# First four FFN units on x times scale, shift and root at their eviction, and two units' split weights in other buffers

## The reference

```
h = rms_norm(x) * (1 + scale) + shift        # scale, shift: per feature, from mod = silu(c) @ mod_w + mod_b
x = x + 0.5 * gate * ((silu(h @ w_g) * (h @ w_u)) @ w_down)      # D_FF = 2816
```

## Time and profile before

| | us |
|---|---|
| median of 3 runs | 1985.31 (1983.57 to 1985.61) |
| the profiled execution's own time | 1985.01 |
| span in the profile | 1983.2 |
| TensorE busy | 1952.4 |
| VectorE busy | 1138.5 |
| ScalarE busy | 716.8 |
| POOL busy | 214.1 |
| start of the first four units / of units 8 and 9 | 20.15 / 72.85 |

### The profile page before, as it was taken

The page is one execution under the profiler, slowest core; times in us unless marked ns, Lnnn a source line. Parts: engine busy times, 40 slices in busy tenths (PEclk is TensorE's granted clock), DMA queues, the critical chain, the costliest instruction groups (busy, mean ns, idle before and its releaser), DMA issues.

```text
span 1983.2 us, 23246 instructions
## 1 busy us (share of the span) xinstructions
PE 1952.4 (98%) x8990; PEld 1619.5 (82%) x8990; DVE 1138.5 (57%) x1692; ACT 716.8 (36%) x1056; POOL 214.1 (11%) x246
## 2 busy tenths in 40 slices
PE   7999999999999999999999999999999999999998
PEld 5888888888888888888888888878888888888886
DVE  7665564799857655645864453586554572433334
ACT  5322222464743213224422221356465442222123
POOL 4110100017701100100110000001111000000000
PEclk9999999999999999999999999999999999999999
DMA  8665552322016655622554543223322233323221
GB/s 318 236 219 170 202 191 96 103 90 88 33 64 223 203 183 187 232 83 87 175 200 136 166 159 108 93 98 112 97 85 86 70 104 97 106 85 106 85 90 59
DMA packets 75197, 263.94 MB, mean 133 GB/s; under 512 B 8770, under 2 KB 8898, under 8 KB 75123
## 3 DMA queue, kind: packets, MB, share of 16 engines
q1 hardware_dynamic: 54720, 190.87, 28.7%
q0 software_dynamic: 20256, 72.02, 11.0%
q10 hardware_dynamic: 146, 0.09, 0.0%
HBM read 260.66 MB, written 2.13 MB: 133 GB/s over the span
## 4 chain that ended last, share of the span: by engine, by line
PE 94%; DVE 3%; POOL 1%; issue 1%; ACT 1%; DMA 0%; SPq 0%; DVEq 0%; ACTq 0%; POOLq 0%
PE bank L1392 29%; PE bank L1397 29%; PE bank L1393 29%; PE bank L1800 1%; DVE dve_tmp L953 1%; PE bank L1817 1%; PE bank L1732 1%; PE bank L1576 1%; DVE h_lo L944 1%; PE bank L1578 1%; PE bank L1577 1%; PE bank L1789 0%; PE bank L1707 0%; PE bank L1456 0%; DVE wlo L816 0%
## 5 line engine op out<-in xcount | busy, mean ns | idle before, releaser
L1392 PE MATMUL bank<-h_hi,whi 128*128 128x512 f32 x1808 | 711.5, 394 | 7.5 <-DVE wlo L816 4.5
L1393 PE MATMUL bank<-h_hi,wlo 128*128 128x512 f32 x1808 | 705.5, 390 | 0.0
L1397 PE MATMUL bank<-h_lo,whi 128*128 128x512 f32 x1808 | 593.9, 390 | 0.5 <-POOL h_lo L378 0.5
L481 ACT ACTIVATE whi<-wraw 128x1024 fp32r<-128x1024 f32 x338 | 347.0, 1053 | 267.0 <-PE bank L1397 263.9
L816 DVE TENSOR_TENSOR wlo<-wraw,whi 128x1024 fp32r<-128x1024 f32 x324 | 389.0, 1224 | 59.9 <-ACT whi L481 59.6
L1392 PEld LDWEIGHTS bank<-h_hi,whi 128*128 128x128 f32 x1808 | 340.7, 188 | 81.0 <-issue 6.1
L1397 PEld LDWEIGHTS bank<-h_lo,whi 128*128 128x128 f32 x1808 | 340.1, 188 | 73.1 <-POOL h_lo L378 1.2
L1393 PEld LDWEIGHTS bank<-h_hi,wlo 128*128 128x128 f32 x1808 | 340.8, 189 | 68.9
L1392 PE MATMUL bank<-hid_hi,whi 128*128 128x512 f32 x832 | 324.3, 390 | 0.0
L1397 PE MATMUL bank<-hid_lo,whi 128*128 128x512 f32 x832 | 323.7, 389 | 0.0
L1393 PE MATMUL bank<-hid_hi,wlo 128*128 128x512 f32 x832 | 323.7, 389 | 0.0
(11 more groups left out here) (237 smaller groups left out, 1351.3 us busy)
## 6 DMA issues: line engine op xcount, KB each, us to landing
wraw<-in_w_units_dram SPq DMA_DIRECT2D x306, 512.0 KB, 3.5
arena<-in_mod_t_dram POOLq DMA_DIRECT2D x96, 512.0 KB, 5.0
mod_tile<-in_mod_t_dram POOLq DMA_DIRECT2D x32, 512.0 KB, 4.8
wraw<-in_w_units_dram SPq DMA_DIRECT2D x32, 384.0 KB, 3.6
arena<-in_mod_t_dram SPq DMA_DIRECT2D x12, 512.0 KB, 8.1
arena<-in_w_units_dram SPq DMA_DIRECT2D x10, 512.0 KB, 4.5
xT<-in_xt_dram SPq DMA_DIRECT2D x8, 256.0 KB, 4.5
sq<-k_roots POOLq DMA_DIRECT2D x8, 256.0 KB, 3.5
```

The lines of the kernel that those rows point to most:

```text
L481: act.activation(whi[:, s % RING, :, :], wraw[:, s % RING, :, :], ACT.Copy).then_inc(hi_ready, 1)
L1392: pe.matmul(dst, whi[:, w, k, :], hi_, start=first, stop=False)
L1393: pe.matmul(dst, wlo[:, w, k, :], hi_, start=False, stop=False)
L1397: return pe.matmul(dst, whi[:, s % RING, k, :], lo_, start=False, stop=last)
```

## The change

1. `first_tile`: all 8 scale columns come first, then the 8 shift columns.
2. Units 0 to 3 run on x * scale without root and shift: ScalarE makes the rounded product (`first_scaled`, L535 of the new file), VectorE its lower part (`first_lower`, L1186). The root is spread by TensorE between the matmuls of these units, behind the part of units 0 and 1 for k = 2, and ScalarE copies it to `ssum` after its fourth scaled column.
3. The shift goes through the weights of units 0 to 3 by 16 matmuls with a 2-row output (L1714), turned into columns by four small ones (L1733). At eviction VectorE multiplies the bank by the root (`first_evict`, L1198); the shift column is the bias of the gate function (L568) and is added in the product (L1080).
4. Units 4 and 5 keep their split weights in the upper halves of `hid_hi` and `hid_lo` (L554 on ScalarE, L388 on POOL, L1227 on VectorE) and have matmuls of their own (`first_pair`), step by step with the pieces of h.
5. h itself is made after that, from `ssum` in place of the bank, with a new buffer in the arena. Units 6 and 7 are raised after it (ScalarE) and split within the gating of hidden tile 1 (VectorE).
6. On TensorE the second pair of pairs in each FFN's first third is written out, and the loop starts one later.

```diff
@@
-    return KT * (1 - t % 2) + t // 2
+    return KT + t if t < KT else t - KT
@@ POOL
+            first_lo(2)
+            first_lo(3)
+            pool.wait_ge(hi_ready, 5)
+            pool.wait_ge(lo_ready, 4)
+            pool.tensor_tensor(first_lo_[0], wraw[:, 0, :, :], first_hi[0].bitcast(F32), ALU.subtract).then_inc(lo_ready, 1)
             for k in range(KT):
-                if k == 1:
-                    first_lo(2)
-                    first_lo(3)
                 pool.wait_ge(h_rounded, k + 1)
-                pool.tensor_tensor(h_lo[:, k, :], sq[:, k % 2, :], h_hi[:, k, :].bitcast(F32), ALU.subtract)\
+                pool.tensor_tensor(h_lo[:, k, :], first_full[k % 2], h_hi[:, k, :].bitcast(F32), ALU.subtract)\
                     .then_inc(h_ready, 1)
@@ ScalarE
             hi(0)
+            first_scaled(0)
             hi(1)
-            first_h(0)
+            first_scaled(1)
             hi(2)
             hi(3)
-            for k in range(1, KT):
+            for k in range(2, KT):
+                first_scaled(k)
+                if k == 3:
+                    act.wait_ge(rb_ready, 1)
+                    act.activation(ssum[:, :], bank[RB], ACT.Copy).then_inc(rb_kept, 1)
+            first_raised(0)
+            first_raised(1)
+            for k in range(KT):
                 first_h(k)
+            act.wait_ge(rows_done, 1)
+            hi(6)
+            hi(7)
             act.wait_ge(mod_done, MOD_FIRST)
             act.activation(cond[:, :], cond_wide, ACT.Copy).then_inc(cond_kept, 1)
             ffn(0, 1)
@@ VectorE, gating of the first FFN
+                        elif f == t == 0 and n < 2:
+                            dve.wait_ge(evicted, s + 2)
+                            dve.wait_ge(shift_kept, 1)
+                            dve.scalar_tensor_tensor(out=dve_tmp[:, n, :], in0=first_out[2 * n + 1],
+                                                     scalar=shift_out[:, 2 * n + 1:2 * n + 2], in1=act_tmp[:, n, :],
+                                                     op0=ALU.add, op1=ALU.mult).then_inc(early_gated, 1)
+                            if n:
+                                lo(6)
+                                lo(7)
@@ VectorE, the start
+            for k in range(2, KT):
+                mod_column(k)
+                dve.wait_ge(mod_done, k + 1)
+                first_lower(k)
+            for t in range(KT, MOD_FIRST):
+                mod_column(t)
+            dve.wait_ge(mod_done, MOD_FIRST)
+            link(dve.tensor_copy(shift_split[:, :, 0], modc[:, 0:KT]))
+            dve.tensor_tensor(shift_split[:, :, 1], modc[:, 0:KT], shift_split[:, :, 0].bitcast(F32), ALU.subtract)\
+                .then_inc(first_shift, 1)
+            dve.wait_ge(rb_kept, 1)
+            first_evict(0)
+            first_evict(1)
             first_norm(0)
-            lo(0)
-            lo(1)
+            dve.wait_ge(hi_ready, 6)
+            dve.wait_ge(lo_ready, 5)
+            dve.tensor_tensor(first_lo_[1], wraw[:, 1, :, :], first_hi[1].bitcast(F32), ALU.subtract).then_inc(lo_ready, 1)
             for k in range(1, KT):
-                mod_column(2 * k)
-                mod_column(2 * k + 1)
                 first_norm(k)
...
+            first_evict(2)
+            first_evict(3)
+            dve.wait_ge(columns_done, 1)
+            dve.tensor_copy(shift_out[:, :], bank[OB][:, 0:4]).then_inc(shift_kept, 1)
+            dve.wait_ge(h_ready, KT)
             dve.wait_ge(cond_kept, 1)
             ffn(0, 1)
@@ TensorE
                         if f == 0:
                             first_units()
+                            first_pair()
+                            pair(6, 0, (2, 3), 4)
                         else:
                             up_body(up, 0, True)
-                        with pe.Fori(0, k // 2 - 1) as i:
-                            up_body(up + 4, i, False)
+                            up_body(up + 4, 0, False)
+                        with pe.Fori(0, k // 2 - 2) as i:
+                            up_body(up + 8, i, False)
@@ TensorE, first_units
                 for k in range(KT):
                     last = part(0, k)
-                    if k:
-                        part(2, k - 1)
                     if k == KT - 1:
                         last.then_inc(unit_done, 2)
+                    if k == 2:
+                        pe.wait_ge(root_ready, 1)
+                        spread(bank[RB], 0, 0).then_inc(rb_ready, 1)
+                    if k:
+                        part(2, k - 1).then_inc(early_used, 1)
                 part(2, KT - 1).then_inc(unit_done, 2)
+                pe.wait_ge(first_shift, 1)
...
```

More of the change, by code:

```diff
@@ L517, in round_h, with first_scaled @@
                                    scale=1.0).then_inc(h_rounded, 1)
+            def first_scaled(k):
+                act.wait_ge(mod_done, k + 1)
+                act.activation(h_hi[:, k, :], xT[:, k, :], ACT.Copy, scale=modc[:, KT + k:KT + k + 1]).then_inc(early_rounded, 1)
             def first_h(k):
@@ L537, in up_body @@
                             s = up + 2 * q
+                            if f == 0 and s < RING and isinstance(i, int):
+                                act.wait_ge(evicted, s + 1)
+                                act.wait_ge(shift_kept, 1)
+                                act.activation(act_tmp[:, q, :], first_out[2 * q], ACT.Silu,
+                                               bias=shift_out[:, 2 * q:2 * q + 1], scale=1.0).then_inc(act_out, 1)
+                                act.wait_ge(early_gated, q + 1)
+                                act.activation(hid_hi[:, q:q + 1, :], dve_tmp[:, q:q + 1, :], ACT.Copy)\
+                                    .then_inc(hid_rounded, 1)
+                                continue
                             if early and q == 0:
@@ L1127, in _, with first_lower @@
             dve.wait_ge(cond_spread, 1)
-            mod_column(0)
-            mod_column(1)
-            spread_rstd(0)
+            def first_lower(k):
+                dve.wait_ge(early_rounded, k + 1)
+                dve.scalar_tensor_tensor(out=h_lo[:, k, :], in0=xT[:, k, :], scalar=modc[:, KT + k:KT + k + 1],
+                                         in1=h_hi[:, k, :].bitcast(F32), op0=ALU.mult, op1=ALU.subtract)\
+                    .then_inc(early_ready, 1)
             def first_norm(k):
-                dve.wait_ge(mod_done, 2 * k + 2)
                 if k >= 2:
@@ L1136, in first_norm, with first_evict @@
                 dve.scalar_tensor_tensor(out=dve_tmp[:, k % 2, :], in0=xT[:, k, :], scalar=modc[:, KT + k:KT + k + 1],
-                                         in1=bank[RB][:, :], op0=ALU.mult, op1=ALU.mult).then_inc(normed, 1)
+                                         in1=ssum[:, :], op0=ALU.mult, op1=ALU.mult).then_inc(normed, 1)
+            def first_evict(n):
+                dve.wait_ge(unit_done, n + 2 - n % 2)
+                dve.tensor_tensor(first_out[n], bank[n], ssum[:, :], ALU.mult).then_inc(evicted, 1)
+            mod_column(0)
+            dve.wait_ge(stat_done, 1)
+            dve.tensor_scalar(var[:, 0, 0:NB], bank[OB][:, 0:NB], 1.0 / D, EPS, ALU.mult, ALU.add).then_inc(var_ready, 1)
+            lo(0)
+            dve.wait_ge(mod_done, 1)
+            first_lower(0)
+            lo(1)
+            mod_column(1)
+            dve.wait_ge(mod_done, 2)
+            first_lower(1)
+            split_roots(0, NB)
+            for k in range(2, KT):
[11 more added lines that the diff above has]
+            first_evict(1)
             first_norm(0)
-            lo(0)
-            lo(1)
+            dve.wait_ge(hi_ready, 6)
+            dve.wait_ge(lo_ready, 5)
+            dve.tensor_tensor(first_lo_[1], wraw[:, 1, :, :], first_hi[1].bitcast(F32), ALU.subtract).then_inc(lo_ready, 1)
             for k in range(1, KT):
-                mod_column(2 * k)
-                mod_column(2 * k + 1)
                 first_norm(k)
+                if k == 4:
+                    dve.wait_ge(rows_done, 1)
+                    dve.tensor_copy(first_rows, bank[OB][0:2, :]).then_inc(rows_kept, 1)
+            first_evict(2)
[3 more added lines that the diff above has]
+            dve.wait_ge(h_ready, KT)
             dve.wait_ge(cond_kept, 1)
@@ L1592, in first_stat @@
                 ins.then_inc(stat_done, 1)
-                pe.wait_ge(root_ready, 1)
-                spread(bank[RB], 0, 0).then_inc(rb_ready, 1)
             def first_units():
@@ L1608, in first_units, with first_pair @@
                     last = part(0, k)
-                    if k:
-                        part(2, k - 1)
                     if k == KT - 1:
                         last.then_inc(unit_done, 2)
-                part(2, KT - 1).then_inc(unit_done, 2)
+                    if k == 2:
[3 more added lines that the diff above has]
+                        part(2, k - 1).then_inc(early_used, 1)
+                part(2, KT - 1).then_inc(unit_done, 2)
```

(25 more changed lines are left out.)

34 lines of the change are left out of this document (25 added, 9 removed).

## The result

The changed kernel takes 2003.11 us (median) where the kernel before, run beside it, takes 1984.44: a ratio of 1.0092, 95% interval 1.0081 to 1.0103, or 18.7 us more. One single run of the six took 9706.79 us and is no part of the ratio. The profiled execution took 2003.35 us, with a span of 2001.6.

What follows compares the result with a forecast made beforehand. TensorE, busy 98%, bounds the kernel through its stands and slow matmuls. Units 8 and 9 begin at 30.5 + 48.8 + 10.9 + 2.5 = 92.7 against 72.85, +19.9 us, so 2005.0 us, range 1998.5 to 2010.5.

Steps and rivals of the forecast that it cites:

- the likeliest case: The chain waits for the splits of units 6 and 7, and VectorE and POOL hold each other: 2005.0 us, chance 0.60.
- T: End of the root's spread on TensorE: 32.8 at the slow level, 29.3 at the fast, taken as 30.5 us.
- stand before the shift's matmuls: TensorE, done with units 0 to 3, stands near 4 us; this decides nothing, as the chain runs on through VectorE.
- wait for the first modulation tile: VectorE before its modulation columns: POOL fetches the tile after its last h_lo, landing 4.9 us after issue, at T + 43.3.
- What starts earlier: Kernel start: TensorE begins near 17.4 instead of 20.15, but units 2 and 3 wait for POOL's splits until 25.6.
- The new chain: From the root's spread through VectorE's columns and shift split to the last h_lo: T + 20.2, then T + 38.4.
- I therefore add VectorE's and POOL's work instead of laying it side by side: Making the eight pieces of h: both engines hold each other, 14.3 us from T + 24.0, done 3.6 us later.
- The rival without holding: VectorE and POOL do not hold each other while making h: +16.0 us, 2001.0 us; chance 0.22.
- The tail: After h: gate, two modulation columns, second product, then VectorE's splits of units 6 and 7, done at T + 48.8.
- The slow level after the long stand: TensorE on units 6 and 7 after standing over 9 us: slow matmuls cost 2.5 us, bounds 0 and 4.4.
- TensorE is the bound after all: Rival: only TensorE's own work counts up to units 8 and 9, +1.3 us, 1986.5 us; chance 0.03.

Runs made afterwards that it cites:

- experiment two: Changed kernel with ScalarE's copy of the root moved behind its last scaled column, nothing else: 1999.01 us, 4.1 us under the changed kernel.
- Experiment one: Changed kernel with VectorE's splits of units 6 and 7 moved ahead of the first gate, nothing else: 1998.36 us, 4.75 us under the changed kernel.
- five to eight: Includes one run not named singly: experiment three plus modulation columns of the first two tiles moved behind the third gate's splits: 1988.89 us, ratio 1.002.
- experiment five: Changed kernel with 30 extra matmuls, read by nothing, on TensorE right ahead of units 6 and 7: 2000.51 us, 2.6 us under the changed kernel.
- experiment seven: Experiment three plus columns of tiles 0 and 1 behind the third gate's splits, and the norm reading the root from its bank: 1987.61 us, ratio 1.0014.
- experiment eight: Changed kernel with units 4 and 5 split into the ring's own buffers, as before the change: 2012.17 us, 9.1 us over the changed kernel.
- experiment three: Changed kernel with both splits of 6 and 7 ahead of the first gate and the root's copy behind the scaled columns: 1991.82 us, ratio 1.0037.
- experiment four: Changed kernel with the norm of the first h reading the root from its bank, not SBUF: 2003.12 us, ratio 1.0093.
- kernel nine: Experiment seven with VectorE's column k+1 ahead of the lower part of k, and the root's split ahead of lower part 1: 1985.47 us, ratio 1.0006.
- ten: Kernel nine with TensorE taking the root's spread and units 0 and 1's third part before units 2 and 3's first part: 1982.71 us, ratio 0.999.

## Why the prediction was right, and where its terms were off

The forecast was 2005.0 (1998.5 to 2010.5), the result 2003.11; the likeliest case is the one that happened. Step by step, with T the end of the root's spread:

| term | predicted | measured |
|---|---|---|
| TensorE begins | 17.4 | 17.22 |
| units 2 and 3's splits | 25.6 | 25.34, after a stand of 3.76 |
| T | 30.5 | 31.5 |
| split of the shift | T + 20.2 | T + 20.6 |
| stand before the shift's matmuls | near 4 | 4.21 |
| last h_lo done | T + 38.4 | T + 37.2 |
| wait for the first modulation tile | 0.8 (T + 42.5 to 43.3) | none, column at T + 41.5 |
| splits of units 6 and 7 done | T + 48.8 | T + 46.9 |
| units 6 and 7 | 10.9 + 2.5 slow | 12.45, so 10.9 + 1.55 |
| units 8 and 9 begin | 92.7 | 90.97 |

- **What starts earlier** held to 0.3 us, with POOL's splits as the limit.
- **The new chain** held. Its hand-overs made a column 2.81 us and not 2.72, which for three columns is 0.3 of the 0.4. That the stand before the shift decides nothing was right: experiment two takes it away, and what it wins is the chain's 5.0 us, as VectorE's splits, not TensorE, are last.
- **T** was mis-sized by 1.0. I had put it nearer to the fast end; in the changed kernel TensorE was at the fast level from 19.95 to the stand of 3.76 us, and the 12 matmuls behind that stand ran at 0.43 but for the last. Part of this is the execution that was traced. In the profiles of one, two and five to eight all of the first 12 matmuls ran at 0.43, the stand was 2.63 us or so, the first 3 to 6 matmuls behind it were fast, and T came 13.6 us after the first matmul; in the changed kernel's, three's, four's and nine's the fast level came before the stand, and T 14.3 to 14.8 after the first matmul. With 13.6 T would have been 30.8. Why a start goes one way or the other stays open.
- **"I therefore add VectorE's and POOL's work instead of laying it side by side"** had the right mechanism (experiments four and eight) and the wrong size. Seven steps took 1.72 us each, not the 1.96 of adding 1.29 and 0.67. It is less than the full sum, 1.2 us in all. Two things were missing: the norm costs 0.4 to 0.55 us beside POOL and not 0.67 (experiment eight's steps, and the 0.55 by which each norm outlasts POOL's piece), and the pace is that of the ring of two pieces, in which it counts once in two steps. In the record of the changed kernel it stands as a longer VectorE instruction (1.78), hardly as a longer one of POOL. The Trainium skill, page "SBUF — State Buffer", section "SBUF: two separate sides", names this holding; by its rule alone the sum would be mine. The rows bear out that the two are coupled, that in experiment eight either can be the one that waits, and that reading the root from the bank frees them; and they show that a step is shorter than the whole sum. The rival without holding, 2001.0, would have needed steps of 1.36; with the bank they are 1.48, as the ring of ScalarE and POOL then limits, which the prediction did not have.
- **The tail** held by order: gate, two columns, gate, splits. Experiment one is worth 7.5 us at that place: 2.6 of the 3.1 us for which VectorE waited for the gate function, and the 5.1 from there to the splits at 76.11, less 0.25 by which the first split ran longer (1.47 for 1.22). The tile landed within 4.35 us of POOL's issue at 68.69, and no column waited; I had taken 4.9.
- **The slow level after the long stand**, 2.5 predicted, measured 1.55 in the trace and 1.4 by experiment five. It came back 2.8 us after the start, not 5. The page "TensorE: Matmul & The Clock Gate", section "Part 1: The HAM clock gate" of the Trainium skill gave the direction, which experiment five confirms; without it 2.5 would have been left out, and the sum would have been 1.55 us too low in place of 0.95 too high at this step.
- **"TensorE is the bound after all"** was rightly small. But its sum, +1.3, was no floor: ten reaches -2.2, since with the spread and a third part ahead of POOL's splits the 3.1 us of waiting shrink to 0.9, and only 10 matmuls run slowly (2.1 us, where I had 4).

The errors cancel in part: +1.0 at T, -1.9 in the chain (1.2 of it h, the rest the tile and hand-overs), -0.95 at the clock, together some -1.8 at units 8 and 9. The medians differ by 18.7 us where the two traces differ by 18.1 at the mark.

## What to carry to other kernels

When a product is made free of a late factor (here the root, pulled to the eviction), look where the factor is copied and who is queued behind the copy: the work had been freed of the root and ScalarE's order tied it back, at 5 us. An early start is worth only what the next stage can take. TensorE began 2.9 us earlier and then stood for 15.9, half of it (7.88) because splits for the stage after stood behind gates and columns in VectorE's program; moving two lines gave 7.5 us there, and each stand that was removed showed the next one until all four had gone. Price a shared resource by what it costs when nothing else is late: the holding of VectorE and POOL was worth 1.3 us with the other stands removed and nothing with them.

## What the runs showed of the hardware that I had not expected

The slow level's length is not the same from stand to stand, nor from run to run of the same start. In the changed kernel TensorE came to 0.23 us a matmul 2.7 us after its first matmul at 17.22, lost it in the stand of 3.76 us, had it back 5.3 us after 25.34, lost it in the stand of 4.21 and had it back 5.6 us after 52.15, lost it in 7.88 and had it back 2.8 us after 78.52. The granted clock of 0.76 from 17.22 to 31.55 is this. The eleven executions of kernel nine differ in the same way: 1985 us at a mean clock of 0.998, 1987.1 to 1988.2 at 0.995 to 0.997, with nothing changed between them. Stands of 2.4 to 2.6 us went either way. Behind the one before 83.70 in experiment one the first three matmuls ran at 0.23 us and the next nine at 0.43; the same was seen behind the stand of 2.63 us before 25.84 in experiment seven:

```profile
25.84 0.50 PE L1487 MATMUL bank<-h_hi,whi 128*128 128x512 f32 x1 [2.63 <-POOL wlo L381]
...
26.65 0.59 PE L1488 MATMUL bank<-h_hi,wlo 128*128 128x512 f32 x1
27.04 1.05 PE L1492 MATMUL bank<-h_lo,whi 128*128 128x512 f32 x2
```

while the stand of 2.40 us in experiment three cost no slow matmul. So a stand's price can come after it, and a gain of 1.5 us ahead of a stretch that starts slow can be half lost in a longer slow part of it, as in experiment four.

Second, VectorE and POOL do not always share the delay. In the changed kernel POOL's pieces take 1.29 to 1.45 us and five of VectorE's eight norms 1.78 for 0.75; in experiment eight both grow, the norms up to 1.42 and POOL's pieces up to 1.76. The recorded time of the held engine grows, with no idle time to show it: a group's mean (1.45 for the eight norms) near twice its usual is what gives it away in such a profile.
